# Tiles of 128 columns or more placed at multiples of 128 bytes in SBUF

## The reference

```python
def _swiglu(x, w_gate, w_up, w_down):
    return (jax.nn.silu(x @ w_gate) * (x @ w_up)) @ w_down

def _layer(x, ffn1_norm, ffn1_w_gate, ffn1_w_up, ffn1_w_down, mix_norm, w_in, ...):
    x = x + MACARON * _swiglu(_rmsnorm(x, ffn1_norm), ffn1_w_gate, ffn1_w_up, ffn1_w_down)
    h = _rmsnorm(x, mix_norm)
    p = h @ w_in
    ...
    x = x + jnp.concatenate([y_a, y_b, y_c], axis=-1) @ w_out
    x = x + MACARON * _swiglu(_rmsnorm(x, ffn2_norm), ffn2_w_gate, ffn2_w_up, ffn2_w_down)
    return x
```

## The kernel before, in words

| tiles | start in bytes | rest modulo 256 |
|---|---|---|
| `gxh`, `gxl` | 32,896 and 49,280 | 128 |
| `whi0`, `wlo0` (the others 4096 further each) | 82,048 and 98,432 | 128 |
| `R`, `acc`, `sq`, `xs`, `sd` | 114,816 and on, 2048 each | 128 |
| `rcol` | 126,528 | 64 |
| `f_hh`, `f_hl` | 128,192 and 173,248 | 192 |
| `m_yh`, `m_yl`, `xa_yh`, `xa_yl` | 128,192 and 144,576 | 192 |
| `xa_mh`, `xa_ml` | 169,152 and 177,344 | 192 |
| `m_ch`, `m_cl` (three tiles each) | 206,016 and 212,160 | 192 |
| `m_xh`, `m_xl` of head 0 | 185,600 and 193,792 | 0 |

## Time and profile before

### The profile page before, as it was taken

The page is one execution under the profiler, slowest core; times in us unless marked ns, Lnnn a source line. Parts: engine busy times, 40 slices in busy tenths (PEclk is TensorE's granted clock), DMA queues, the critical chain, the costliest instruction groups (busy, mean ns, idle before and its releaser), DMA issues.

```text
span 3464.6 us, 36172 instructions
## 1 busy us (share of the span) xinstructions
PE 3310.8 (96%) x14679; PEld 2685.9 (78%) x14679; DVE 1651.6 (48%) x2054; ACT 987.6 (29%) x1268; POOL 1463.0 (42%) x598
## 2 busy tenths in 40 slices
PE   8999999999999999999999778999999879999997
PEld 6888877888888887788888546778888657778886
DVE  4442476544144414665431756345431775354432
ACT  3222332222222223322222352322222543332221
POOL 4444434444444444344445203444445234344442
PEclk9999999999999999999999889999999989999999
DMA  3222322322332233223223102223223223222221
GB/s 135 98 98 95 116 79 79 103 98 91 110 100 96 97 104 108 73 91 104 98 98 98 64 25 82 95 86 104 98 98 104 70 70 107 92 92 95 97 99 68
DMA packets 91413, 321.54 MB, mean 93 GB/s; under 512 B 10224, under 2 KB 12656, under 8 KB 90992
## 3 DMA queue, kind: packets, MB, share of 16 engines
q1 hardware_dynamic: 85392, 309.45, 27.1%
q10 hardware_dynamic: 5856, 9.79, 0.8%
HBM read 317.10 MB, written 2.10 MB: 92 GB/s over the span
## 4 chain that ended last, share of the span: by engine, by line
PE 87%; DVE 9%; ACT 2%; issue 1%; DMA 1%; SPq 0%; DVEq 0%; ACTq 0%
PE bank L310 27%; PE bank L306 27%; PE bank L307 27%; PE bank L588 1%; PE bank L568 1%; PE bank L500 1%; DVE m_xc L1648 1%; PE bank L413 0%; PE bank L407 0%; PE bank L332 0%; DVE m_xc L1642 0%; DVE m_yl L1156 0%; PE bank L519 0%; DMA xa_mem<-memT 0%; ACT m_pr L836 0%
## 5 line engine op out<-in xcount | busy, mean ns | idle before, releaser
L1766 POOL TENSOR_TENSOR wlo<-raw,whi 128x1024 fp32r<-128x1024 f32 x588 | 1461.7, 2495 | 1969.8 <-ACT whi L655 1969.8
L306 PE MATMUL bank<-gxh,whi 128*128 128x512 f32 x2848 | 1127.2, 396 | 6.3 <-ACT whi L655 6.3
L307 PE MATMUL bank<-gxl,whi 128*128 128x512 f32 x2848 | 1112.5, 391 | 0.0
L655 ACT ACTIVATE whi<-raw 128x1024 fp32r<-128x1024 f32 x588 | 611.0, 1053 | 632.9 <-PE bank L310 620.6
L310 PE MATMUL bank<-gxh,wlo 128*128 128x512 f32 x2848 | 703.3, 389 | 0.0
L306 PEld LDWEIGHTS bank<-gxh,whi 128*128 128x128 f32 x2848 | 537.5, 189 | 126.1 <-issue 9.3
L307 PEld LDWEIGHTS bank<-gxl,whi 128*128 128x128 f32 x2848 | 537.3, 189 | 118.1 <-issue 7.1
L310 PEld LDWEIGHTS bank<-gxh,wlo 128*128 128x128 f32 x2848 | 534.6, 188 | 111.0
L306 PE MATMUL bank<-f_hh,whi 128*128 128x512 f32 x1056 | 413.6, 392 | 0.0
L307 PE MATMUL bank<-f_hl,whi 128*128 128x512 f32 x1056 | 413.2, 391 | 0.0
L1108 DVE SCALAR_TENSOR_TENSOR xs<-bank,x 128x512 f32<-128x512 f32 x96 | 66.4, 692 | 694.7 <-PE bank L310 694.4
(11 more groups left out here) (310 smaller groups left out, 2598.4 us busy)
## 6 DMA issues: line engine op xcount, KB each, us to landing
raw<-stream SPq DMA_DIRECT2D x588, 512.0 KB, 3.3
m_dk<-decay ACTq DMA_DIRECT2D x2, 1024.0 KB, 6.0
xa_mem<-memT ACTq DMA_DIRECT2D x2, 1024.0 KB, 5.6
outT<-x ACTq DMA_DIRECT2D x1, 2048.0 KB, 7.4
x<-xT ACTq DMA_DIRECT2D x4, 256.0 KB, 4.8
x<-xT SPq DMA_DIRECT2D x4, 256.0 KB, 5.6
m_ct<-cos ACTq DMA_DIRECT2D x2, 256.0 KB, 2.7
m_sn<-sin ACTq DMA_DIRECT2D x2, 256.0 KB, 3.0
```

Of the source, the lines that this page charges most:

```text
L306: pe.matmul(out, seq(hi, k, P), h, start=first and k == 0, stop=False)
L307: pe.matmul(out, seq(hi, k, P), l, start=False, stop=False)
L655: act.activation(M.whi[r][:, :], M.raw[r][:, :], ACT.Copy).then_inc(*S.tick("hi", u))
L1766: pool.tensor_tensor(M.wlo[r][:, :], M.raw[r][:, :], M.whi[r][:, :].bitcast(F32), ALU.subtract).then_inc(*S.tick("lo", u))
```

## The change

The function that lays out a tile asks for a start at a multiple of 128 bytes where the tile has 128 columns or more, and of 32 bytes as before where it has fewer:

```diff
@@ -181,7 +181,7 @@
     def sb(self, name, cols, dt=F32):
-        return self.stack.enter_context(self.nc.sbuf_tensor(name, [P, cols], dt))
+        return self.stack.enter_context(self.nc.sbuf_tensor(name, [P, cols], dt, align_bytes=128 if cols >= P else 32))
```

## The result

| | before | changed |
|---|---|---|
| median of 6 runs | 3465.57 us (3464.08 to 3466.8) | 3482.89 us (3481.97 to 3483.66) |
| ratio, 95% interval | | 1.005 (1.0038 to 1.0062) |
| profiled execution, its span | 3466.07, 3464.6 us | 3482.76, 3481.4 us |
| mean granted TensorE clock | 0.980 | 0.981 |

The change makes the kernel 17.3 us, 0.5%, slower. The forecast was 3486.4 us, 21.0 us slower.

The account below looks back on a forecast made before the run. TensorE's start-to-start matmul distance was taken to bound the kernel. Terms 13.9 + 3.4 + 1.7 + 0.3 + 1.7 = +21.0 us on a 3465.4 us median gave 3486.4 us, range 3464 to 3491.

Parts of the forecast that it names:

- Where it bounds: In stages with big products, time is the number of matmuls times the start-to-start distance on TensorE, busy 96%.
- Down projections, +13.9 us: SwiGLU down projections: 3168 matmuls with f_hh, f_hl slow from 228.9 to 233.3 ns, +13.9 us.
- Output projections, +5.1 us: Output projections, 4.4 ns more per matmul: mixers 768 matmuls, +3.4 us; cross attentions 384, +1.7 us.
- `product3`, +0.3 us: Small products with m_ch and the pooling weights: 60 matmuls counted, +0.3 us; m_xh stays at rest 0, nothing.
- 256 columns, +1.7 us, guessed as half: Cross attentions' xa_mh, xa_ml: 768 matmuls at 2.2 ns, half the 512-column price, +1.7 us; bounds 0 and +3.4.
- gx, 0 us: Gate and up products, 8544 matmuls: neither operand moves, so nothing changes; three steps stay at 32.64 us.
- the pair in the earlier trace: In product3 before the change, m_ch matmuls 228.9 ns apart and m_xh 233.3, with the same lines and weight-piece pattern.
- any rule with a period within 2048 bytes: Any address rule repeating within 2048 bytes, own address or distance from weights, gives moved f and m_y tiles m_xh's 233.3 ns.
- Aligned is fast: Rival, chance 0.11: rule is modulo 128, all stage tiles reach gx's 226.7 ns; 3455 us.
- No effect: Rival, chance 0.11: matmul distance depends on stage, memory traffic or unit order, not addresses; time stays 3465.4 us.
- A step of a different size: Rival, chance 0.08: rest 0 is slow, but f_hh settles between 229 and 233 ns; half step, +10 us, 3476 us.

Follow-up runs that it names:

- e1: Kernel before with all stage tiles 192 bytes further, every moving operand at rest 128 modulo 256 like gx; 3457.65 us, ratio 0.9976.
- e7: As e1, with the cross attentions' 256-column memory tiles 192 bytes further, at rest 64; 3456.72 us, ratio to the kernel before 0.9976.
- e2: Kernel before with padding ahead of weights and blocks: whi at rest 192, wlo 0, gx unmoved, stage tiles 128 (m_xh, m_xl 192); 3525.70 us, one run.
- e5: As e1, with gx, weight buffers and all stage tiles 64 bytes further, every start at rest 192 modulo 256; 3458.71 us, one run.
- e6: Kernel before with the four weight slots at rests 128, 192, 0 and 64, moving operands at 128 (m_xh 192); 3494.18 us, one run.
- e9: The change's own edit with 256 in place of 128, all tiles of 128 columns or more at rest 0; 3457.64 us, ratio to kernel before 0.9973.
- e3: Kernel before with only the six SwiGLU blocks' tiles moved, f_hh and f_hl at rests 224, 32, 64, 96, 128, 160; 3476.95 us, one run.
- e10: e3 run once more, unchanged; 3477.19 us.

## Why the prediction was right, point by point

- **Where it bounds.** TensorE's pace from start to start sets the time: right. Of the 16.8 us by which the span grew, the busy time of TensorE has 14.7, and VectorE, the only other one with more, 1.6.
- **Down projections, +13.9 us.** 228.9 to 233.3 ns was forecast and found, and 3168 x 4.4 = 13.9 us stands. Summed over all starts of `f_hh` and `f_hl` matmuls, the two traces differ by 13.9 us.
- **Output projections, +5.1 us.** The first, second and fourth mixer show 233.3. The third mixer and both cross attentions come to 232.4 and not 233.3, as in the first cross attention, second and eighth output tile (VectorE's timeline of the changed kernel):

```profile
2304.83 0.69 DVE L1108 SCALAR_TENSOR_TENSOR xs<-bank,x 128x512 f32<-128x512 f32 x1 [2.77 <-PE bank L310]
...
2338.29 0.69 DVE L1108 SCALAR_TENSOR_TENSOR xs<-bank,x 128x512 f32<-128x512 f32 x1 [2.75 <-PE bank L310]
```

  33.46 us for six units, 232.4 ns. Summed over all: +4.2 us. The prediction speaks of three mixers. There are four, with 192 of these matmuls each; its 768, three lines of 256, are right.
- **`product3`, +0.3 us.** 27 matmuls with `m_ch` take 6.28 us (2014.03 to 2020.31) where 6.30 was forecast. `m_xh` keeps its pace, 4.20 us for 18 (2753.51 to 2757.71), though its rest modulo 2048 went from 1280 to 1536; its distance modulo 256 did not change.
- **256 columns, +1.7 us, guessed as half.** Units take 2.78 to 2.88 us in place of 2.83; the sum is +1.0 us, within the bounds of 0 and 3.4.
- **gx, 0 us.** Right: 32.64 us both times.
- **Not in the sum.** Some 3.4 us came back in the cross attentions. The first eight matmuls of L588 for a pair of heads took 5.35 us in all four pairs before; in the changed kernel they take 3.65 in two of the four. The second pair on the chain of waits, before and changed:

```profile
2273.24 5.35 PE bank L588 x8
...
2284.55 3.65 PE bank L588 x8
```

  The granted clock over these stretches (columns as in the earlier trace rows) was 0.68 before and 1.00 in the changed kernel:

```profile
2273.20:2278.60 5.40, 5.38 (x10) 2.33 (x11) 2.10 (x5) 0.00 (x0) 0.00 (x0) 0.68 0.00 0
...
2284.50:2288.20 3.70, 3.67 (x10) 1.74 (x11) 1.91 (x5) 0.00 (x0) 0.00 (x0) 1.00 0.00 0
```

  Before, part of these matmuls ran at 1.2 GHz and the others at 2.4; in the changed kernel all ran at 2.4. Nothing was tried to show whether the addresses or the timing of the stages brought that about. The number of slow pairs varies from run to run: three of four in e1, four in e7.
- **Added up.** For the two profiled executions 13.9 + 4.2 + 1.0 - 3.4 = +15.7 us. The first matmul starts 0.8 us later (14.97 in place of 14.20), and the span grew by 16.8. The matmul terms alone gave 19.1 of the 20.7 us that were forecast for them, so the size was right by its terms; the clock's 3.4 us were in no term and moved the total the other way.
- **The reasoning behind the size** was right in its result and half wrong in its ground. I took the address of the moving operand for the cause, since the two readings (its own rest, or its distance from the weights) gave the same here. e2, e5, e6 and e9 decide for the distance, and with it the pair in the earlier trace rows: `m_ch` stood at +64 and `m_xh` at 128. The sentence that any rule with a period within 2048 bytes gives the 233.3 ns of `m_xh` is what carried the forecast, and it covered both.
- **Rivals.** "Aligned is fast" would have needed the tiles at the same distance as `gx`; alignment to 128 leaves open whether that is 0 or 128, and here it was 128. "No effect" is refuted by e1, where only addresses moved and the same stage went to 226.7 ns. The Trainium skill (TensorE: Matmul & The Clock Gate, Back-to-back issue gap) gives N / 2.4 + 2.5 = 215.8 ns for 512 columns, as the gap of isolated matmuls and with no address in it. It doesn't describe these fp32r streams, which show values from 226.7 to 237 ns at one clock. "A step of a different size" was not far off for the cross attentions, 3.5 ns in place of 4.4, but not for `f_hh`, which took the full step.

## What to carry to other kernels

Where fp32r matmuls of 512 columns bound a kernel, read the distance from start to start in several stages: two stages with the same shape and the same clock and a different distance are a hint at addresses. Put the moving and the stationary operand at starts that are equal modulo 256 bytes, the simplest way being 256 for both (e9, 0.9973 of the time); alignment to 32, 64 or 128 bytes leaves that to chance, and here it was the wrong chance. The gain over the kernel before is a quarter of a per cent, since its two distances happened to be the best ones of the map. Don't carry it to other widths or formats unmeasured: with 256 columns equal starts were not the best.

## What the runs showed of the hardware that I had not expected

- That the cause lies in two addresses together. Moving only the weights (e2) slowed matmuls whose activations had not moved from 226.7 to 232.8 ns, by the starts 47 us over all matmuls with `gx`.
- That the map has no slope: 226.7 ns at 0, 237 at 4 bytes, 228.9 at +64, 233 at -64, and 232 to 235 elsewhere.
- That one distance can have two rhythms: 228.9 and 233.3 ns at +64, where the same program showed the one in one execution and the other in the next (e3, e10); 232.4 and 233.3 at 128 in the changed kernel; 113.3 and 117.9 for 256 columns at -64 (e7).
- That at the half clock (1.2 GHz) none of it shows: 426 ns for 512 columns at distance 128, and as much at distance 0 (e1, `m_xh`, six matmuls in 2.56 us from 2711.57 to 2714.13). An explanation would be two streams of reads that get in each other's way only at the full rate. That is argued from this and from the map; the runs show the dependence, not the mechanism, and not what picks one of the two rhythms.
